# A hybrid decoder step on one core: rows served ahead, gate one-hots on GpSimd, norm roots by Ln and Exp, attention and state space steps reordered

## What is computed

```python
h = rmsnorm(x, norm_mix);  q, k, v, z, xbc, dt = split(h @ w_in)
# differential attention, 8 heads, two maps of 64 each; q and k are RMS-normed
a = softmax(s)[:, :, 0] - lam * softmax(s)[:, :, 1];  o = rmsnorm(a @ v, subln) * (1 - lam0)
# Mamba-2 state space part: causal conv, silu, 16 heads of 64, state 128, chunks of 128
y, state = ssd_scan(xs, dtv, A, Bm, Cm, ssm_prev);  y = rmsnorm((y + d_skip * xs) * silu(z), ssm_norm)
x = x + concat(o, y) @ w_out
# cross-attention on 256 memory tokens, 4 heads of 128; q and memory keys are RMS-normed
x = x + softmax(qx @ mem_k) @ mem_v @ wo_x
# PEER: 8 heads pick 16 of 128 x 128 experts each through product keys
s  = q . keys                       # two lists of 128, top 16 of each, top 16 of the 256 sums: eid, g
act = gelu(t . u_tab[eid]);  x = x + sum((g * act) * v_tab[eid])
```

## Time and profile before

| | |
|---|---|
| median of 3 runs | 3928.59 us (3925.68 to 3934.28) |
| the profiled execution | 3938.14 us, its span 3936.5 us |
| mean granted clock of TensorE | 0.94 of full speed |
| HBM traffic | 1051 MB read, 36 MB written; 276 GB/s over the span |

### The profile page before, as it was taken

How to read it: one execution, slowest core, us unless ns; L and a number is a source line. 1 busy time by engine, 2 the same in 40 slices (tenths; PEclk the granted TensorE clock), 3 DMA queues, 4 the chain that set the end, 5 groups by cost and what they waited for, 6 DMA issues and landing times.

```text
span 3936.5 us, 41100 instructions
## 1 busy us (share of the span) xinstructions
PE 3546.1 (90%) x15837; PEld 2905.5 (74%) x15837; DVE 2500.9 (64%) x4048; ACT 535.7 (14%) x1049; POOL 804.8 (20%) x645
## 2 busy tenths in 40 slices
PE   8988887998988887978987799999998999999999
PEld 6765444876777676856776687887887887888887
DVE  4444655534877646657868589666665665666666
ACT  2232222021123322020123100000000000000000
POOL 0000110000011112210000244223323323322233
PEclk9988888987999899988998899999999999999999
DMA  4333545452367656854444799999999999999999
GB/s 168 124 122 123 182 165 182 147 169 93 120 252 257 221 187 231 334 220 150 160 172 182 286 368 369 415 414 409 408 414 376 414 414 397 406 414 417 415 405 379
DMA packets 217893, 1090.49 MB, mean 277 GB/s; under 512 B 23075, under 2 KB 64291, under 8 KB 112099
## 3 DMA queue, kind: packets, MB, share of 16 engines
q0 software_dynamic: 89680, 595.47, 38.5%
q1 hardware_dynamic: 125570, 475.09, 31.9%
q10 hardware_dynamic: 2448, 17.30, 1.1%
HBM read 1051.29 MB, written 36.47 MB: 276 GB/s over the span
## 4 chain that ended last, share of the span: by engine, by line
PE 65%; DVE 18%; DMA 7%; SPq 3%; issue 3%; ACT 3%; POOL 1%; DVEq 0%; ACTq 0%
PE pj L310 21%; PE pst L1943 17%; PE pj L1976 17%; SPq L2073 3%; DVE gs L1887 3%; DMA gs<-in_peer_v,arena 3%; DMA ring<-in_up 2%; PE pst L964 1%; DMA gs<-in_peer_u,arena 1%; DVE arena L561 1%; DVE arena L1040 1%; DVE arena L1041 1%; DVE acc L1895 1%; PE pj L1573 1%; DVE arena L2017 1%
## 5 line engine op out<-in xcount | busy, mean ns | idle before, releaser
L1943 PE MATMUL pst<-hb,ring 128*128 128x264 f32 x4096 | 946.4, 391 | 36.1 <-DMA ring<-in_up 33.2
L1976 PE MATMUL pj<-arena,ring 128*128 128x264 f32 x4096 | 935.5, 388 | 26.9 <-DVE arena L1966 13.1
L1943 PEld LDWEIGHTS pst<-hb,ring 128*128 128x128 f32 x4096 | 787.2, 193 | 176.1 <-DMA ring<-in_up 36.7
L1976 PEld LDWEIGHTS pj<-arena,ring 128*128 128x128 f32 x4096 | 782.7, 191 | 162.6 <-DVE arena L1966 13.3
L1895 DVE SCALAR_TENSOR_TENSOR acc<-gs,arena,acc 128x2048 f32<-128x2048 f32 x256 | 601.6, 2350 | 215.9 <-DMA gs<-in_peer_v,arena 209.8
L1928 POOL DMA_INDIRECT gs<-in_peer_u,arena x256 | 378.1, 1477 | 1545.3 <-DVE arena L1887 1342.8
L1887 DVE CUSTOM_DVE_ANT_0 gs<-gs,hnat 128x2048 f32<-128x2048 f32 x256 | 586.3, 2290 | 123.6 <-DMA gs<-in_peer_u,arena 108.8
L310 PE MATMUL pj<-hb,ring 128*128 128x256 f32 x2048 | 482.5, 392 | 8.9 <-DVE hb L265 7.8
L1928 POOL DMA_INDIRECT gs<-in_peer_v,arena x256 | 346.1, 1352 | 699.2 <-DVE acc L1895 651.9
L310 PE MATMUL pj<-gs,ring 128*128 128x264 f32 x1792 | 457.4, 410 | 7.1 <-DVE gs L265 5.7
L310 PEld LDWEIGHTS pj<-hb,ring 128*128 128x128 f32 x2048 | 396.4, 197 | 73.3 <-issue 15.9
(11 more groups left out here) (418 smaller groups left out, 2690.3 us busy)
## 6 DMA issues: line engine op xcount, KB each, us to landing
ring<-in_w SPq DMA_DIRECT2D x160, 1024.0 KB, 4.8
ring<-in_up SPq DMA_DIRECT2D x128, 1024.0 KB, 9.9
ring<-in_down SPq DMA_DIRECT2D x256, 512.0 KB, 10.7
xb<-in_cache_k POOLq DMA_DIRECT2D x32, 512.0 KB, 5.3
xb<-in_cache_v POOLq DMA_DIRECT2D x32, 512.0 KB, 3.5
gates<-mix ACTq DMA_DIRECT2D x16, 1024.0 KB, 3.9
mix<-gates SPq DMA_DIRECT2D x16, 1024.0 KB, 21.0
arena<-in_state_ssm POOLq DMA_DIRECT2D x8, 512.0 KB, 9.6
```

The source lines that it names most:

```text
L1943: m = pe.matmul(pst[:, j % 2, 0:TD], ring[:, j % 2, c * P:(c + 1) * P], hb[:, c, :], start=(c == 0), stop=(c == DC - 1))
L1976: m = pe.matmul(sums(n), value_tile(n)[:, k * P:(k + 1) * P], wt[:, r % SLOTS * EG + k, :], start=(k == 0), stop=(k == EG - 1))
```

## The change

It has five parts. (1) All roots of norms: ACT computes Ln of scale x sum + eps straight from PSUM, then Exp of -0.5 times that; DVE's scale-and-add and its reciprocals go. (2) In attention PE's steps of a head stand later among the quarters, ACT's order follows, and DVE's rows are split over six places. (3) In the state space pairs the steps become functions and are reordered; the samples' last transposes move to the next pair; small sums move to another PSUM tile; `opvs` is a new SBUF tile. (4) 202 rows instead of 100 are served ahead: 7 per attention step of B, 6 per pair, 24 at the output projection as before, 2 per cross head, 12 at wo, 3 per late-keys head, 30 behind the last pick; the first Gelu of the rows moves ahead of B's cross-attention. (5) The one-hots are made on POOL, 8 `tensor_scalar` of 128 x 128 per chunk, in one program with the gathers; the first 33 chunks stand behind up tiles 3 to 13, three each, the others behind 15 to 23, four each.

The diff, cut to its core:

```diff
+            act.wait_ge(s_sqsum, DC // 2 + k)
+            hold(act, s_root, k)
+            act.activation(nrt[:, 0:cols], pst[:, 0, 0:cols], ACT.Ln, bias=eps, scale=1.0 / D).then_inc(s_var, 1)
             act.wait_ge(s_var, k + 1)
-            act.activation(nrt[:, 0:cols], nrt[:, 0:cols], ACT.Sqrt).then_inc(s_root, 1)
...
-            dve.wait_ge(s_sqsum, DC // 2 + k)
-            dve.tensor_scalar(nrt[:, 0:cols], pst[:, 0, 0:cols], 1.0 / D, EPS, ALU.mult, ALU.add).then_inc(s_var, 1)
             dve.wait_ge(s_root, k + 1)
-            o.step(dve.reciprocal(nrstd[:, 0:cols], nrt[:, 0:cols]))
...
+            def attend(step, *args):
+                if do_att:
+                    step(*args)
+
             quarter(0, 0)
-            if do_att:
-                values()
-                scores(0)
+            attend(values)
             quarter(0, 1)
+            attend(scores, 0)
             quarter(0, 2)
-            if do_att:
-                scores(1)
             quarter(0, 3)
-            if do_att:
-                transposes(0)
+            attend(scores, 1)
             quarter(1, 0)
-            if do_att:
-                pv(0)
+            attend(transposes, 0)
             quarter(1, 1)
+            attend(pv, 0)
             quarter(1, 2)
-            if do_att:
-                transposes(1)
             quarter(1, 3)
-            if do_att:
-                pv(1)
             quarter(2, 0)
+            attend(transposes, 1)
             if do_proj:
                 qk_sums(0)
-            if do_att:
-                out_sums()
             quarter(2, 1)
+            attend(pv, 1)
             if do_proj:
                 qk_sums(1)
             quarter(2, 2)
+            attend(out_sums)
             quarter(2, 3)
 
...
+                    act.wait_ge(s_qksum, 2 * G + j + 1)
+                    act.activation(rt2[:, j, 0:cols], pst[:, j, 0:cols], ACT.Ln, bias=eps,
+                                   scale=1.0 / AD).then_inc(s_qkvar, 1)
+                for j in range(2):
                     act.wait_ge(s_qkvar, 2 * G + j + 1)
-                    act.activation(rt2[:, j, 0:cols], rt2[:, j, 0:cols], ACT.Sqrt).then_inc(s_qkroot, 1)
+                    act.activation(rt2[:, j, 0:cols], rt2[:, j, 0:cols], ACT.Exp, scale=-0.5).then_inc(s_qkroot, 1)
...
                 exps(0)
-                exps(1)
                 copy_map(0)
             if do_proj:
                 copy_out(0)
                 squares(0)
             if do_att:
+                exps(1)
+            if do_proj:
+                copy_out(1)
+                squares(1)
+            if do_att:
                 copy_map(1)
                 act.wait_ge(s_pv, 2 * at_ + 2)
                 act.activation(osq, pov[:, 0:GT], ACT.Square).then_inc(s_osq, 1)
             if do_proj:
-                copy_out(1)
-                squares(1)
+                roots()
             if do_att:
+                act.wait_ge(s_osum, at_ + 1)
+                act.activation(ort, ptr[:, 0:GT], ACT.Ln, bias=eps, scale=1.0 / P).then_inc(s_ovar, 1)
                 act.wait_ge(s_ovar, at_ + 1)
-                act.activation(ort, ort, ACT.Sqrt).then_inc(s_oroot, 1)
+                act.activation(ort, ort, ACT.Exp, scale=-0.5).then_inc(s_oroot, 1)
             if do_proj:
-                roots()
                 copy_out(2)
 
...
-            def mean_square(j):
-                dve.wait_ge(s_qksum, 2 * G + j + 1)
-                dve.tensor_scalar(rt2[:, j, 0:cols], pst[:, j, 0:cols], 1.0 / AD, EPS, ALU.mult,
-                                  ALU.add).then_inc(s_qkvar, 1)
-
             def normed(j, dst, gain, s):
                 dve.wait_ge(s_qkroot, 2 * G + j + 1)
-                o.step(dve.reciprocal(rt2[:, j, 0:cols], rt2[:, j, 0:cols]))
                 if j == 0:
...
                 block(0)
-                rows_dve(dve, o, rows // 4)
+                rows_dve(dve, o, rows[1])
                 block(1)
-            rows_dve(dve, o, rows // 2)
+            rows_dve(dve, o, rows[3])
             if do_proj:
-                mean_square(0)
+                normed(0, qn, pr("q_norm"), s_qn)
+                normed(1, kn, pr("k_norm"), s_kn)
+            rows_dve(dve, o, rows[4])
             if do_att:
-                dve.wait_ge(s_osum, at_ + 1)
-                dve.tensor_scalar(ort, ptr[:, 0:GT], 1.0 / P, EPS, ALU.mult, ALU.add).then_inc(s_ovar, 1)
                 dve.wait_ge(s_oroot, at_ + 1)
-                o.step(dve.reciprocal(ort, ort))
                 dve.scalar_tensor_tensor(out=mix[:, g - 1, 0:GT], in0=pov[:, 0:GT], scalar=sub8[:, 0:1], in1=ort,
                                          op0=ALU.mult, op1=ALU.mult).then_inc(s_omix, 1)
             if do_proj:
-                mean_square(1)
-                normed(0, qn, pr("q_norm"), s_qn)
-                normed(1, kn, pr("k_norm"), s_kn)
                 if gi == 0:
...
+            sampled = ssd and gi == 0
+            quarter(0, 0)
+            if sampled:
+                if s % (NP_ // 2):
+                    sample_turned(s - 1)
+                sample_rows()
+            quarter(0, 1)
+            if ssd:
+                broadcast()
+            quarter(0, 2)
+            if ssd:
+                turned()
+            quarter(0, 3)
+            quarter(1, 0)
+            if ssd:
+                states()
+            quarter(1, 1)
+            if sampled:
+                sample_max()
+            quarter(1, 2)
+            if sampled:
+                sample_shift()
+            if ssd:
+                outputs()
+            if sampled:
+                sample_sums()
+            quarter(1, 3)
+            if sampled:
+                sample_values()
+                if s % (NP_ // 2) == NP_ // 2 - 1:
+                    sample_turned(s)
...
+            if ssd and gi == 0:
+                if s % (NP_ // 2):
+                    sample_out(s - 1)
+                products(0)
+                inputs()
+                products(1)
+                gaps()
+                products(2)
+                decayed()
+                products(3)
+                sample_max()
+                carried()
+                sample_diag()
+                sample_state()
+                sample_shift()
+                sample_update()
+                sample_weights()
+                mixed()
+            elif ssd:
+                inputs()
+                rows_dve(dve, o, nrows[0])
+                gaps()
+                decayed()
+                rows_dve(dve, o, nrows[1])
+                carried()
+                rows_dve(dve, o, nrows[2])
+                mixed()
             if proj:
                 been_read(dve, gi, "zx", i, 0)
                 if ssd:
                     dve.wait_ge(s_ymix, S + 1)
                 convolve(o, dve, gi, i, xs)
...
         ROWS = 4 * P
-        R_ATT, R_SSD, R_CROSS, R_WO = 4, 3, 1, 4
+        R_ATT, R_SSD, R_CROSS, R_WO = (1, 1, 1, 1, 2, 1), (2, 1, 2, 1), 2, 12
         R_OUT = tuple(1 + n % 2 for n in range(DC))
-        R_SEL = tuple(hd % 2 for hd in range(PH))
-        R_GATE = tuple(int(q % 8 == 7) for q in range(NQ))
-        BEFORE = AH * R_ATT + NP_ * R_SSD + XH * R_CROSS + R_WO + sum(R_OUT) + sum(R_SEL) + sum(R_GATE)
-        assert BEFORE < P
+        R_SEL, R_GATE = 3, 30
+        OUT_END = AH * sum(R_ATT) + NP_ * sum(R_SSD) + sum(R_OUT)
+        HEADS_END = OUT_END + XH * R_CROSS + R_WO
+        BEFORE = HEADS_END + PH * R_SEL + R_GATE
+        assert OUT_END >= P and BEFORE < 2 * P
...
-        def gates_dve(dve, o, q):
+        def gates_pool(pool, q):
 
             if q == 0:
-                dve.wait_ge(s_trc, 3)
-                dve.wait_ge(s_hout, 16)
-            hold(dve, s_gm, q - 1)
-            per = lambda v: v.rearrange("p (t n) -> p t n", n=P)
-            low, high = per(hots[:, q % 2 * 2, :]), per(hots[:, q % 2 * 2 + 1, :])
-            iota = co("iota")[:, None, :].broadcast_to([P, 4, P])
-            value = lambda i: flat[:, i, 4 * q:4 * q + 4][:, :, None].broadcast_to([P, 4, P])
-            o.step(dve.tensor_tensor(high, iota, value(0), ALU.is_equal))
-            o.last(dve.tensor_tensor(low, iota, value(1), ALU.is_equal))
-            o.step(dve.tensor_tensor(high, high, value(2), ALU.mult))
-            dve.sem_inc(s_hot, 1)
+                pool.wait_ge(s_hout, 16)
+                pool.wait_ge(s_trc, 1)
+            if q == NQ_HALF:
+                pool.wait_ge(s_trc, 3)
+            hold(pool, s_gm, q - 1)
+            for i in range(4):
+                t, n = 4 * q + i, slice(i * P, (i + 1) * P)
+                pool.tensor_scalar(hots[:, q % 2 * 2, n], co("iota"), flat[:, 1, t:t + 1], None,
+                                   ALU.is_equal).then_inc(s_hot, 1)
+                pool.tensor_scalar(hots[:, q % 2 * 2 + 1, n], co("iota"), flat[:, 0, t:t + 1], flat[:, 2, t:t + 1],
+                                   ALU.is_equal, ALU.mult).then_inc(s_hot, 1)
 
         def gates_pe(pe, q):
```

(88 more changed lines are left out.)

243 lines of the change are left out of this document (121 added, 122 removed).

## The result

The changed kernel takes 4159.72 us (median of 4 runs, 4154.45 to 4161.23), the kernel before 3930.75 beside it: ratio 1.0581, interval 1.0563 to 1.0599. The forecast was 3950 in a range of 3862 to 4048. The direction (slower) held, the size did not: +229 us came, +22 was forecast. The profiled execution took 4158.6 us, +220 on that of before.

What follows compares the result with a forecast made beforehand. PE waits for short DVE and ACT chains ahead of the dense steps, and almost only for DMA in them. Terms -12 - 3 - 6 - 8 + 10 + 18 + 76 - 53 = +22 gave 3950 us, range 3862 to 4048.

Steps and rivals of the forecast that it cites:

- the price of the one-hot instruction: Gates on POOL: 528 instructions at 0.31 us each, first down tile at 2288 against 2212, +76 us.
- the rival "dear": POOL one-hots cost 0.45 us or more each: total 4025 and up, 4151 at 0.69; chance 0.18.
- The lock: POOL stands while DVE reads two SBUF operands: 2.0, then 2.3 us per gather; rival without it for one-hots 3848, chance 0.07.
- The dense steps: From the first down tile on, 102 more rows served ahead remove waits for tiles and DVE: -53 us.
- The stages ahead: Stages before the first up tile: roots -12, attention -3 and -6, pairs -8 and +10, wo +18.
- roots and orders: Norm roots -12 us, reordered attention -3 in A and -6 in B, reordered state space pairs of A -8.
- That +10: State space pairs of group B: 24 more DVE rows, pair pitch from 21.4 to 22.7 us, +10 us.
- group A's cross-attention: Four cross heads with two roots each: two reciprocals go against one more table load, -2.3 us each, -9.2 in all.
- The samples' new places in group A: State space pairs of A: products interleaved, sample steps spread over quarters, pitch 38.65 to 36.6-37.6 us, -8 us.
- The wo step: Output step of group B, filled by DVE without a gap: 8 more rows at 2.29 us, +18 us.
- Group B's attention: PE no longer stands for exponentials, but a new 2.4 us wait for the last copy; 29.5 us per group, -6 us.
- the rival in which they share a set: Ln and Exp share a table, so no load between them in B's attention and at 13 roots: 3913 us; chance 0.05.

Runs made afterwards that it cites:

- 160 ahead: The changed kernel with one-hots made by DVE, 8 rows among the late keys and 4 among the gates: 3903.38 us, 0.9924 of the kernel before.
- The version with 127 ahead: Changed kernel with one-hots on DVE, chunk products between up-tile matmuls, fewer rows in B's pairs, wo, late keys and gates: 3816.15 us, 0.9705 of the kernel before.
- the version with 100 rows ahead: Changed kernel with one-hots on DVE, few rows among keys and gates, group B's row counts as before: 3884.36 us, 0.9883 of the kernel before.

## Why the prediction was wrong

**The step that failed is the price of the one-hot instruction.** "With a pitch like its neighbours' I take 0.31" was read from DVE's row of the same shape; the runs show 0.59 for the compare and 0.79 for compare and multiply, 0.69 on average. 528 x (0.69 - 0.31) = 201 us, and the miss of the stage is 198. The bound of 0.69 stood in the text as its upper end, with 4151 as its price, and was met: the rival "dear" (4025 and up) had 0.18 and the range ended at 4048. That the bound was met so closely is chance: it is DVE's price of another shape, and the runs' 0.69 is the mean of two prices. The trace of before had no row of POOL computing, so nothing in it made 0.31 more likely than 0.69. The Trainium skill (GPSIMD Engine Reference, "Elementwise — side-by-side cycle accounting") has 1.8 cycles an element at best, by its 1.2 GHz an estimate of 0.19 us for 128 columns. The measured prices lie far above it: by the same clock the two sizes give 3.0 cycles a column for one operation and about 4 for two, on the fixed part of 0.27 and 0.35 us.

**What held of that step.** The lock of the earlier trace rows does hold for one-hots. The forecast used 2.0 and 2.3 us of standing and 1.24 of gather for each row; a run with 50 rows fewer puts both at 2.9 together. In the changed kernel's trace the 528 one-hots take 462.6 us, 100 more than 264 x (0.589 + 0.786) at their median pitches, where 108 of standing was forecast (24 x 2.0 + 26 x 2.3), and the 50 gathers take 59, where 62 was. The rest of the stage's miss is at its end: PE waits 23.2 us for the gates of the first step, where 13.1 was taken. That POOL's chain sets the first down tile, that 0.1 us moves it by 53, and that nothing covers it are all as written. The first part is 32 chunks and the second 34, not 33 and 33, which changes next to nothing in the sum.

**The dense steps** were forecast at 1666 us and took 1654.6, with no wait for the ring: right in mechanism, and 10 us better. But the prediction had one sum for all 102 rows, and their worth is uneven. From 100 to 160 ahead the steps fall by 50 us (0.8 a row), from 160 to 202 by 7 (0.16 a row). The version with 127 ahead, which differs in its early stage too, has 39 of the 50 already, at a DMA share of 1.01.

**The stages ahead** came out at +10 where -1 was forecast, by errors that partly cancel. In the version with 100 rows ahead the first up tile starts 43 us earlier than before, but 30 of these are the pairs of group B; the rest is 13, where the forecast had 29 in gains of roots and orders. The 60 rows outside keys and gates cost 61 us where they are served, against 28 forecast (10 in the pairs, 18 at wo). In the pairs the order, the rows' places above all, won 30 us (167.4 to 137.8) and the rows took 36 back. That +10 was forecast and +6.1 measured is luck in part, a small difference of two terms that the forecast did not have apart. Of the -9.2 in group A's cross-attention 3 came.

The samples' new places in group A were to win 8 us. The pitches of its pairs did fall by 2 in sum, though the fourth rose from 52.1 to 55.2 us, but the last pair with the end of the stage got 4.6 longer, so that the row of the table is +2.4. Which step does that was not tried. The wo step (+18.7 for +18), by its row, is within 1 us.

Group B's attention was to win 6 us and lost 2. Its steps are 29.5 to 31.2 us apart, and one 42.2, as one of 40.7 was before. PE's waits in it say why:

```profile
PE ptr L386 <- ACT arena L494: 18.5, 7, 4.1
PE pst L401 <- ACT arena L475: 14.9, 4, 9.1
```

The new wait for the last copy (L494) came as forecast, 2.6 us a time for 2.4. What failed is that PE would no longer stand for the exponentials (L475): 14.9 us of that are left, of 17.2 before.

**Loads between Ln and Exp** stand in the trace of the changed kernel too; the rival in which they share a set is out for this build. ACT in one attention step of group B:

```profile
1219.76 1.28 ACT L503 ACT_TABLE_LOAD   x1
1221.06 0.84 ACT L503 ACTIVATE arena<-pst,lam 128x256 f32<-128x256 f32 x2
1221.91 1.28 ACT L507 ACT_TABLE_LOAD   x1
1223.21 0.72 ACT L507 ACTIVATE arena<-arena 128x256 f32<-128x256 f32 x2
1223.94 1.28 ACT L533 ACT_TABLE_LOAD   x1
1225.24 0.47 ACT L533 ACTIVATE arena<-ptr,lam 128x256 f32<-128x256 f32 x1
1225.73 1.28 ACT L535 ACT_TABLE_LOAD   x1
1227.03 0.42 ACT L535 ACTIVATE arena<-arena 128x256 f32<-128x256 f32 x1
1227.35 0.36 ACT L494 ACTIVATE arena<-pj 128x256 f32<-128x256 f32 x1
```

Four loads, 5.1 us, stand ahead of the last copy (L494), as the prediction had it.

In one sum, from the medians: roots, orders and the rows' new places -46, the 60 rows of group B's stages +19 net of the dense steps (3884 to 3903), the 42 rows among keys and gates +86, the one-hots on POOL +170: +229.

## What to carry to other kernels

Price work that moves to another engine from a run on that engine; where no row of it exists, let the range reach the far bound, which here was the right one. Rows of work served early paid here only while DMA was the bound later on: count how many it takes until the matrix engine is no longer idle there, and stop. And one piece of filler work between two links of a chain hides what three in one place do not.

## What the runs showed of the hardware that was not expected

A GpSimd `tensor_scalar` on 128 partitions, float32, took 0.43 us for 64 columns and 0.59 for 128 with one operation, and 0.57 and 0.79 with two. An estimate from these is 0.27 us and 2.5 ns a column, and 0.35 us and 3.4 ns. DVE takes 0.29 us for a scalar operation on 128 columns. One such GpSimd instruction that meets a DVE row of 128 x 2048 with two SBUF inputs (some 2.4 us) stood for 1.7 to 1.9 us of it and took 2.28 to 2.67 us. PE, waiting for it, was granted 0.67 and 0.73 of its clock over 540 us, a mix of its two levels, where the same 66 chunks on DVE between the up tile's matmuls ran at 0.94 (the version with 127 rows ahead).
